# Adding two slabs of gathered expert rows to the residual: both additions on VectorE, none on GpSimd

## What is computed

```python
def hierarchical_moe(h, ...):            # h (512, 1024)
    ...                                   # two experts and two weights per token
    for e in range(N_EXPERTS):
        y = (jax.nn.silu(h @ w_gate[e]) * (h @ w_up[e])) @ w_down[e]
        out = out + combine[:, e:e + 1] * y.astype(jnp.float32)
    return out

def hybrid_layer(x, ...):
    ...
    y = hierarchical_moe(h2, ...)
    return x + y.reshape(B, S, -1).astype(x.dtype)

def reference(x, ...):
    x = hybrid_layer(x, ...)
    return rms_norm(x, final_norm_g)
```

## Time and profile before

| what | value |
|---|---|
| median of 3 runs | 606.22 us (606.18 to 608.25) |
| span of the profiled execution, first to last instruction (no other time of it is given) | 606.8 us |
| TensorE busy | 574.4 us, 95% of the span |
| VectorE busy | 421.0 us, 69% |
| ScalarE busy | 349.9 us, 58% |
| GpSimd busy | 135.7 us, 22% |
| mean granted TensorE clock | 0.989 |
| chain that ended last, by engine | TensorE 83%, VectorE 7%, DMA 4%, nobody waited for ("issue") 2%, ScalarE 2%, SP's queue 1%, GpSimd 1% |

### The profile page before, as it was taken

How to read it: one execution, slowest core, us unless ns; L and a number is a source line. 1 busy time by engine, 2 the same in 40 slices (tenths; PEclk the granted TensorE clock), 3 DMA queues, 4 the chain that set the end, 5 groups by cost and what they waited for, 6 DMA issues and landing times.

```text
span 606.8 us, 8244 instructions
## 1 busy us (share of the span) xinstructions
PE 574.4 (95%) x2859; PEld 471.2 (78%) x2860; DVE 421.0 (69%) x559; ACT 349.9 (58%) x457; POOL 135.7 (22%) x116
## 2 busy tenths in 40 slices
PE   4799999999999999997999999999999999999973
PEld 3689878888887888885878888888888888888851
DVE  3811466552683764365399898889989889989857
ACT  4722343585023432350577888878788878788623
POOL 4410000000000000014604442233443233411170
PEclk9999999999999999999899999999999999999997
DMA  8995222022210046796199999999999999993163
GB/s 300 379 372 196 71 69 68 4 69 71 71 45 26 7 167 231 244 397 239 62 311 374 375 372 371 362 374 374 366 389 372 373 372 370 354 384 132 46 251 139
DMA packets 72140, 144.85 MB, mean 239 GB/s; under 512 B 3906, under 2 KB 13290, under 8 KB 71984
## 3 DMA queue, kind: packets, MB, share of 16 engines
q1 hardware_dynamic: 65936, 125.49, 58.5%
q0 software_dynamic: 6176, 19.00, 9.0%
HBM read 132.89 MB, written 14.71 MB: 243 GB/s over the span
## 4 chain that ended last, share of the span: by engine, by line
PE 83%; DVE 7%; DMA 4%; issue 2%; ACT 2%; SPq 1%; POOL 1%; POOLq 0%; DVEq 0%; ACTq 0%
PE ps L1222 23%; PE ps L1224 22%; PE ps L1223 22%; PE ps L1229 5%; DMA arena<-w_in 2%; PE ps L1287 2%; PE ps L1264 2%; PE ps L1237 2%; PE ps L1324 1%; PE ps L1312 1%; DMA arena<-y_dram 1%; PE ps L1278 1%; DVE res L1183 1%; PE ps L1351 1%; DVE act_lo L832 1%
## 5 line engine op out<-in xcount | busy, mean ns | idle before, releaser
L1222 PE MATMUL ps<-hi_ring,act_hi 128*128 128x512 f32 (+1 forms) x608 | 240.9, 396 | 1.2 <-DVE act_lo L832 1.2
L1022 DVE TENSOR_TENSOR lo_ring<-arena,hi_ring 128x2048 fp32r<-128x2048 f32 x94 | 215.1, 2291 | 37.7 <-ACT hi_ring L737 36.6
L1224 PE MATMUL ps<-hi_ring,act_lo 128*128 128x512 f32 (+1 forms) x608 | 233.9, 385 | 0.0
L1223 PE MATMUL ps<-lo_ring,act_hi 128*128 128x512 f32 (+1 forms) x608 | 233.7, 384 | 0.0
L737 ACT ACTIVATE hi_ring<-arena 128x2048 fp32r<-128x2048 f32 x94 | 180.1, 1917 | 20.8 <-PE ps L1224 14.8
L1222 PEld LDWEIGHTS ps<-hi_ring,act_hi 128*128 128x128 f32 x608 | 114.6, 188 | 28.4 <-issue 6.0
L1224 PEld LDWEIGHTS ps<-hi_ring,act_lo 128*128 128x128 f32 x608 | 114.4, 188 | 23.5
L1223 PEld LDWEIGHTS ps<-lo_ring,act_hi 128*128 128x128 f32 x608 | 114.7, 189 | 20.4
L823 DVE TENSOR_TENSOR lo_ring<-arena,hi_ring 128x512 fp32r<-128x512 f32 x68 | 44.9, 686 | 48.3 <-ACT hi_ring L613 47.8
L537 POOL DMA_INDIRECT y_dram<-y,row_info x15 | 16.1, 1072 | 154.8 <-issue 154.8
L832 DVE TENSOR_TENSOR act_lo<-ps,act_hi 128x512 fp32r<-128x512 f32 x64 | 41.5, 682 | 12.3 <-ACT act_hi L775 5.9
(11 more groups left out here) (178 smaller groups left out, 530.5 us busy)
## 6 DMA issues: line engine op xcount, KB each, us to landing
arena<-w_gate SPq DMA_DIRECT2D x32, 1024.0 KB, 12.2
arena<-w_up SPq DMA_DIRECT2D x32, 1024.0 KB, 12.7
arena<-w_down SPq DMA_DIRECT2D x32, 1024.0 KB, 12.5
arena<-w_in SPq DMA_DIRECT2D x16, 512.0 KB, 9.1
y_dram<-arena POOLq DMA_DIRECT2D x8, 512.0 KB, 11.3
arena<-w_out SPq DMA_DIRECT2D x4, 1024.0 KB, 5.1
arena<-y_dram SPq DMA_DIRECT2D x8, 512.0 KB, 7.4
arena<-w_in SPq DMA_DIRECT2D x3, 1024.0 KB, 15.7
```

The source lines that it names most:

```text
L1022: nc.vector.tensor_tensor(lo(N1 + n12), raw(n12), hi(N1 + n12).bitcast(F32), ALU.subtract).then_inc(lo_done, 1)
L1222: nc.tensor.matmul(dst, a_hi, b_hi, start=start, stop=False)
L1223: nc.tensor.matmul(dst, a_hi, b_lo, start=False, stop=False)
L1224: return nc.tensor.matmul(dst, a_lo, b_hi, start=False, stop=stop)
```

## The change

GpSimd's four additions go. VectorE waits for the two slabs itself and adds first one and then the other to the residual. The semaphore `y_added` stays, now raised by VectorE's first addition and waited for by its second, which reads what the first has written.

```diff
             pool.wait_ge(meta_sent, 16 * 2 * T)
-
-            def add_pairs():
-
-                for t in range(T):
-                    pool.wait_ge(y_in[t], 32)
-                    nc.gpsimd.tensor_tensor(raw(t)[:, 0:D], raw(t)[:, 0:D], raw(t)[:, D:2 * D],
-                                            ALU.add).then_inc(y_added, 1)
-
-            long_lists(pool, traffic_unit, first=lambda: scatter(1, E - 1), after=add_pairs, otherwise=add_pairs)
+            long_lists(pool, traffic_unit, first=lambda: scatter(1, E - 1))
...
             def add_rows(t):
                 v = res_t[:, t, :]
+                dve.wait_ge(y_in[t], 32)
+                nc.vector.tensor_tensor(v, v, raw(t)[:, 0:D], ALU.add).then_inc(y_added, 1)
                 dve.wait_ge(y_added, t + 1)
-                return nc.vector.tensor_tensor(v, v, raw(t)[:, 0:D], ALU.add)
+                return nc.vector.tensor_tensor(v, v, raw(t)[:, D:2 * D], ALU.add)
```

## The result

The changed kernel takes 604.12 us, the median of five runs (602.69 to 604.39), and the kernel before beside it 606.95 us (606.18 to 608.25). The ratio is 0.9947, with a 95% interval of 0.9928 to 0.9965. By the ratio, which is formed over all runs of both kernels and not from the two medians, that is 3.2 us less (2.1 to 4.4); the medians themselves lie 2.8 us apart. That the kernel got faster at all is clear of the noise. A second set of runs, further down, gave 0.9943 (0.9922 to 0.9963).

What follows compares the result with a forecast made beforehand. VectorE's tail additions, taking turns with GpSimd's, were held to be on the path. L1209 of tile 0 gains 4.69 us, less about 1.25 given back: 606.8 - 3.43 = 603.4; median 0.6 lower, 602.8 us, range 602.0 to 604.2.

Steps and rivals of the forecast that it cites:

- The turns: Tail: VectorE's and GpSimd's slab additions run alternately, not side by side, stretching VectorE's from 1211 up to 3357 ns.
- The arithmetic of 2.35 + 1.0: Tail: a long addition is one short one of its own plus what remained of the other engine's, making 3.35 us.
- The price of a pair: VectorE's two chained additions per tile: 1.25 us from first to second, next instruction 1.14 us after the second's start.
- The order of time: Tail, tile by tile: VectorE's L1209 of tile 0 starts at 587.54 instead of 592.23, 4.69 us earlier.
- the landing of the third pair: Tile 2's second slab, the sixth load, lands at 585.1; VectorE's first addition on it starts at 585.15.
- The term: Tail: L1209 of tile 1 starts at 591.07 instead of 594.50, 3.43 us earlier; the rest to the end unchanged.
- What is given back: Between L1209 of tiles 0 and 1, tile 3's extra addition costs about 1.25 us; tiles 0 and 1 cost nothing.
- 0.2 early: TensorE's placing of tile 3 at 1.2 GHz throughout: there at 595.9, wanted by VectorE's L1209 at 596.11.
- late loads: Rival, tail: slab loads become the bound, each microsecond of third-pair delay costing one; 603.8 us with 1 us; chance 0.10.
- slow additions: Rival, tail: VectorE's additions take 3.3 us for their own reasons, not GpSimd's doing; 610.9 us; chance 0.04.
- The drift: Rival, rest of the program: rebuild and execution differences partly cover the tail's gain; 603.2 to 604.5 us; chance 0.10.
- the prediction's last sign: Ahead of 574 us: the prediction is wrong if anything there has moved by more than a few tenths.

Runs made afterwards that it cites:

- the shadow additions: Changed kernel with GpSimd again adding each tile's two slabs, into memory nobody reads and nobody waiting: 609.9 us, ratio 1.005.
- the second pair of traces: Kernel before and changed kernel, each run again without edit: tails from last send to end 36.57 and 32.07 us, ratios 0.9988 and 0.9943.
- the one at 566.22: Changed kernel with tile 3's two slab additions moved from VectorE to TensorE, as identity products into PSUM: 601.9 us, ratio 0.991.
- The one addition of GpSimd's that was worth its while here: Changed kernel with GpSimd summing tile 3's slabs and TensorE adding that sum into PSUM: 601.25 us, ratio 0.9897.

## Why the prediction was right

*The turns.* Read from two long additions and a gapless GpSimd, and shown by the shadow additions: 3.25 to 3.37 us each beside GpSimd, 1.22 without it. The arithmetic of 2.35 + 1.0 held. Not all of the gain is turns: in the kernel before each sum also goes over GpSimd first. No run parts the two. An estimate from the rows: with the third pair there at 585.15 and no turns, GpSimd's 2.39 and VectorE's 1.14 us would bring L1209 of tile 0 to 588.7. It began at 592.23 and was forecast at 587.54, so of the 4.69 us some 3.6 are turns and 1.1 the way over GpSimd.

*The price of a pair.* 1.25 us from first to second and 1.14 behind it were forecast, 1.25 to 1.26 and 1.14 to 1.15 measured. A wait for the engine's own result does cost 0.1 us here, against the sentence of the Trainium skill (VectorE: DVE Perf Modes, "The DRAIN you can't avoid") that I weighed.

*The order of time.* L1209 of tile 0 was forecast 4.69 earlier and came 5.02 earlier (17.12 against 22.14 after the last send). The size that was off is the landing of the third pair: it was assumed 15.0 us after the last send, and VectorE began that pair 0.3 us sooner than I had it in the first trace and 1.3 sooner in the second, where the pair ahead of it was the bound almost as much. The term stood at 3.43 us to L1209 of tile 1; it was 3.76, and by the second pair of traces 4.0, to which the lost clock of that trace adds 0.5.

*What is given back.* 1.26 us for tile 3, nothing for tiles 0 and 1, as forecast, by the two kernels that leave additions out. Tile 2's extra addition lies on the path in the timeline too; no run took it out.

*TensorE.* Here a step failed, though nothing hung on it. I wrote that at the lower clock tile 3 would be there "0.2 early", and looked at tile 3 alone, from the changed kernel's side. In the kernel before it was tile 2 that came 0.28 us late in one of two traces. So the kernel before lost up to 0.5 us that the change returns, and my sum didn't have it.

*The time.* Forecast 602.8 us in 602.0 to 604.2; measured 604.12, 0.08 us inside the upper end and outside the 602.3 to 603.5 that the terms allowed. That the time still fell into the range is luck in part. The difference was forecast as 3.4 us, and measured as 3.2 (2.1 to 4.4; 2.8 by the medians) and 3.5. The time itself is higher mostly because the kernel before came out at 606.95 in five runs where three had given 606.22. One assumption was loose: I set the profiled span of 606.8 against the median of 606.22 as if both stood for the same execution. The changed kernel's profiled execution has a span of 601.8 and a time of 604.28, 2.5 more; by that the first trace of the kernel before was of one of its longer executions. Since I took a difference within the tail, this did no harm.

The rivals: late loads and slow additions did not come about. The drift did, with a last send that moved between 566.2 and 570.1 us in the traces here, and it is what makes a gain of 3.8 us in the tail hard to see in the times. By the prediction's last sign, nothing ahead of 574 us moved by more than a few tenths, it would have been wrong: the last send moved by 1.24 us. The sign was badly chosen, for the kernel before moved by 1.76 from one execution to the next. The twelve traces show where the drift arises. In the middle of the kernel TensorE stands still for 3.2 to 4.2 us and starts again between 285.2 and 286.4 us; in eleven of the traces its granted clock falls to 0.50 during this standstill or just behind it, for 6.8 us in the four with the last send at 568.85 to 570.09, for 3.4 us in the seven at 567.46 to 568.34, and not at all in the one at 566.22. Take off from each last send the time at which TensorE starts again and half of the time at the lower level, which is what half the clock costs a busy TensorE, and 0.9 of the 3.9 us of drift is left. Before and changed both had the 6.8 us in their first traces, and 1.21 of the 1.24 us between them is that TensorE started again at 286.44 in the one and 285.23 in the other. Why the standstill ends earlier or later, and why the clock falls after it for longer or shorter, was not tested.

## What to carry to other kernels

Work put on a second engine isn't parallel if both engines need the same way into memory: look for instructions of one shape with two durations, and ask what ran on the other engine. The one addition of GpSimd's that was worth its while here was the one beside which VectorE read one input from PSUM. When moving work onto a busy engine, count only what doesn't fall into its waits for loads: of the additions moved, tile 3's cost its full price and those of tiles 0 and 1 nothing, as long as the loads landed no earlier. And where executions drift by more than the change is worth, measure the trace from the last event that the change can't touch.

## What was not expected of the hardware

GpSimd's fills (0.93 us each) ran beside VectorE's two-input additions at full speed, so not all of GpSimd's work takes turns. TensorE's granted clock fell to its lower level during standstills of 4.9 and 5.6 us in the kernel before. It was back 2.8 us after the late placings began in the first trace (8 records in 5.09 us) and 5.5 us after in the second (6.44 us), and tile 2 was in time in the one and 0.28 us late in the other: the same program lost nothing in one execution and 0.5 us in the other. In the tails of the kernels here whose late placings stood still for 1.54 us or less, the clock stayed at 1.00 until the last placing was done.
